# First norm's modulation: the last four of sixteen row tiles of quarters two to four multiplied and summed on TensorE

## The reference, cut to what matters

```
mod = silu(c) @ w_ada[l] + b_ada[l]            # w_ada is 2048 x 12288
shift1, scale1, gate1, shift2, scale2, gate2 = jnp.split(mod[:, None, :], 6, axis=-1)
h    = rmsnorm(x, norm_mix_g[l]) * (1 + scale1) + shift1
proj = h @ w_in[l]
```

## Time and profile before

| | |
|---|---|
| median of 3 runs | 2436.21 us (2435.95 to 2436.79) |
| profiled execution, its own time | 2439.67 us |
| its span in the profile | 2437.8 us |
| mean granted clock of TensorE | 0.97 |
| PE busy | 2305.4 us (95%), weight loads 1919.4 us (79%) |
| DVE busy | 964.6 us (40%) |
| ACT, POOL busy | 716.3 us (29%), 926.5 us (38%) |
| DMA | 355.46 MB, mean 146 GB/s |

### The profile page before, as it was taken

One profiled execution on the slowest core, in us unless ns is written; L12 is line 12 of the kernel. 1 busy time (PEld: TensorE's weight loads), 2 busy tenths in 40 slices (PEclk: granted clock), 3 DMA queues, 4 the chain that ended last, 5 costly groups with the idle time before them and its releaser, 6 DMA issues.

```text
span 2437.8 us, 27141 instructions
## 1 busy us (share of the span) xinstructions
PE 2305.4 (95%) x10448; PEld 1919.4 (79%) x10448; DVE 964.6 (40%) x1380; ACT 716.3 (29%) x980; POOL 926.5 (38%) x438
## 2 busy tenths in 40 slices
PE   3778899899998899999999999999999999999999
PEld 3667778687886788788888888888888888888887
DVE  5869886656524467496211012011021021111112
ACT  3134343433335422232122122222132231221221
POOL 1013333243431154344444444444444444444442
PEclk7889999999998999899999999999999999999999
DMA  9865445454536377256333333322333322333332
GB/s 339 308 231 168 152 160 177 167 193 156 217 104 241 108 290 259 87 201 239 107 101 96 95 95 97 100 95 95 95 95 103 95 95 95 95 103 95 95 113 78
DMA packets 188701, 355.46 MB, mean 146 GB/s; under 512 B 13258, under 2 KB 40396, under 8 KB 187344
## 3 DMA queue, kind: packets, MB, share of 16 engines
q1 hardware_dynamic: 179840, 331.34, 40.7%
q10 hardware_dynamic: 8784, 23.07, 2.5%
HBM read 327.09 MB, written 27.28 MB: 145 GB/s over the span
## 4 chain that ended last, share of the span: by engine, by line
PE 80%; DVE 10%; issue 3%; DMA 3%; ACT 2%; SPq 1%; POOL 1%; ACTq 0%; DVEq 0%; POOLq 0%
PE ps L681 26%; PE ps L683 26%; PE ps L682 25%; DVE acc L1550 2%; DVE yc L1723 2%; DVE accx L1675 1%; DMA araw<-in_w_ada 1%; PE ps L715 1%; DMA wraw<-in_w_in 1%; DMA arawx<-in_w_ada 1%; DMA gb<-g_d 0%; DMA mk<-qk_d 0%; ACTq L1244 0%; DVE utmp L1565 0%; PE ps L895 0%
## 5 line engine op out<-in xcount | busy, mean ns | idle before, releaser
L309 POOL TENSOR_TENSOR wlo<-wraw,whi 128x1024 fp32r<-128x1024 f32 (+2 forms) x372 | 893.1, 2404 | 1314.2 <-ACT whi L304 1306.0
L304 ACT ACTIVATE whi<-wraw 128x1024 fp32r<-128x1024 f32 x376 | 391.8, 1046 | 1235.6 <-PE ps L683 1182.6
L681 PE MATMUL ps<-h2T,whi 128*128 128x512 f32 x1024 | 399.8, 390 | 2.5 <-DVE h2T L2049 2.5
L682 PE MATMUL ps<-h2T,whi 128*128 128x512 f32 x1024 | 399.4, 390 | 0.0
L683 PE MATMUL ps<-h2T,wlo 128*128 128x512 f32 x1024 | 399.3, 390 | 0.0
L681 PE MATMUL ps<-ah,whi 128*128 128x512 f32 x1024 | 398.9, 390 | 0.0
L683 PE MATMUL ps<-ah,wlo 128*128 128x512 f32 x1024 | 398.4, 389 | 0.0
L682 PE MATMUL ps<-al,whi 128*128 128x512 f32 x1024 | 398.4, 389 | 0.0
L2074 DVE TENSOR_TENSOR sq<-utmp 128x512 f32<-128x512 f32 x64 | 71.9, 1142 | 561.3 <-ACT utmp L1487 550.9
L2096 DVE SCALAR_TENSOR_TENSOR x1T<-ps,M,x1T 128x512 f32<-128x512 f32 x128 | 87.5, 744 | 512.7 <-PE ps L683 512.7
L1550 DVE SCALAR_TENSOR_TENSOR acc<-araw,silc,acc 128x512 f32<-128x512 f32 x240 | 227.2, 1008 | 18.0 <-DMA araw<-in_w_ada 17.9
(11 more groups left out here) (284 smaller groups left out, 2582.7 us busy)
## 6 DMA issues: line engine op xcount, KB each, us to landing
wraw<-in_w_ff SPq DMA_DIRECT2D x256, 512.0 KB, 3.6
araw<-in_w_ada SPq DMA_DIRECT2D x128, 512.0 KB, 5.9
wraw<-in_w_in SPq DMA_DIRECT2D x72, 512.0 KB, 6.6
arawx<-in_w_ada SPq DMA_DIRECT2D x64, 512.0 KB, 4.1
wraw<-in_w_out SPq DMA_DIRECT2D x32, 512.0 KB, 6.9
xnat<-in_x ACTq DMA_DIRECT2D x4, 1024.0 KB, 8.3
xT_d<-xT ACTq DMA_DIRECT2D x1, 4096.0 KB, 13.3
qk_d<-sth ACTq DMA_DIRECT2D x16, 256.0 KB, 2.6
```

The source lines that it names most:

```text
L304: act.activation(whi[:, slot, 0:kb, 0:cols], wraw[:, slot, 0:kb, 0:cols], ACT.Copy).then_inc(hi_ready, 1)
L309: pool.tensor_tensor(wlo[:, slot, 0:kb, 0:cols], wraw[:, slot, 0:kb, 0:cols], whi[:, slot, 0:kb, 0:cols].bitcast(F), ALU.subtract).then_in ...
L681: pe.matmul(dst, lhs[0], rhs[0], start=start, stop=False)
L682: pe.matmul(dst, lhs[0], rhs[1], start=False, stop=False)
```

## The change

For the second, third and fourth quarter (q = 1, 2, 3) the row tiles 12 to 15, that is the units of u2 = 6 and 7, are no longer taken by DVE. A new function `ada_products` on PE takes them as they lie in `araw`: each 128 by 128 piece is the weight operand, the matching column of `silc` the moving one, and four row tiles accumulate into one output column. These are 2 (w) x 4 (column groups of 128) x 4 (row tiles) = 32 matmuls a quarter, into columns 8 to 15 of bank 7. They stand behind the waits for `ada_read` and `kv_part` and ahead of `ada_sum`, which stays with its eight matmuls into columns 0 to 7. DVE adds both groups of eight columns to the bias in two dependent instructions, each over shift and scale together, where two independent ones stood.

A quarter now has 24 steps on DVE in place of 32 for q = 1 to 3, and all counts of `ada_step` behind it are shifted (`ada_steps_to`). The slots of units 12 to 15 of the second and third quarter are now free only when PE has read them, so that the loads of units 4 to 7 of the third and fourth quarter wait for `ada_summed` of the quarter before.

```
--- before.py
+++ after.py
@@ -309,9 +309,17 @@
         pool.tensor_tensor(wlo[:, slot, 0:kb, 0:cols], wraw[:, slot, 0:kb, 0:cols],
                            whi[:, slot, 0:kb, 0:cols].bitcast(F), ALU.subtract).then_inc(lo_ready, 1)
 
+    def ada_steps_to(pair):
+
+        return 32 * pair - 8 * min(max(pair - 1, 0), 3)
+
     def ada_unit_release(pair, u):
 
-        return 32 * pair + 4 * (u // 2) + 3 + u % 2
+        return ada_steps_to(pair) + 4 * (u // 2) + 3 + u % 2
+
+    def by_products(pair, u2):
+
+        return pair in (1, 2, 3) and u2 >= 6
 
 
 
@@ -364,7 +372,9 @@
         sp.dma_start(wgate[:, :, :], w_in3[:, :, DIN - 16:DIN]).then_inc(gate_loaded, 16)
 
         def ada_load(pair, u, col0, col1, slots, raw, loaded):
-            if u >= slots:
+            if 4 <= u < slots and pair in (2, 3):
+                sp.wait_ge(ada_summed, pair)
+            elif u >= slots:
                 sp.wait_ge(ada_step, ada_unit_release(pair, u - slots))
             elif not (isinstance(pair, int) and pair == 0):
                 sp.wait_ge(ada_step, ada_unit_release(pair - 1, u + 16 - slots))
@@ -399,7 +409,7 @@
         def ada_unit(d):
 
             for w in range(2):
-                sp.wait_ge(ada_step, 128 + (4 * (d - 1) + 3 + w if d else 0))
+                sp.wait_ge(ada_step, ada_steps_to(4) + (4 * (d - 1) + 3 + w if d else 0))
                 if d == 0:
                     sp.wait_ge(ada_summed, 4)
                 k0 = 2 * (d % 8)
@@ -492,7 +502,7 @@
         sp.wait_ge(blk_done, q_at(PAIRS - 1) + 2)
         heads_load(0)
         pair_fills(PAIRS - 1, 10, PAIR_FILLS + 1)
-        sp.wait_ge(ada_step, 32 * 8)
+        sp.wait_ge(ada_step, ada_steps_to(8))
         sp.wait_ge(g_stored, 16)
         rows_load(0)
         for s in range(2):
@@ -707,9 +717,20 @@
                                      [act_of(i, kt) for i in range(2)], first, last)
             ins.then_inc(blk_done, 1)
 
+        def ada_products(pair, bank):
+
+            for w in range(2):
+                for u2 in (6, 7):
+                    pe.wait_ge(ada_loaded[(2 * u2 + w) % 8], 16 * (2 * pair + 2))
+                for j in range(4):
+                    for kt in range(12, KT):
+                        pe.matmul(ps[:, bank, 8 + 4 * w + j:9 + 4 * w + j],
+                                        araw[:, (2 * (kt // 2) + w) % 8, kt % 2, j * P:(j + 1) * P],
+                                        silc[:, kt:kt + 1], start=(kt == 12), stop=(kt == KT - 1))
+
         def ada_sum(pair, tile, bank):
 
-            pe.wait_ge(ada_step, 32 * (pair + 1))
+            pe.wait_ge(ada_step, ada_steps_to(pair + 1))
             for w in range(2):
                 for j in range(4):
                     ins = pe.matmul(ps[:, bank, 4 * w + j:4 * w + j + 1],
@@ -750,6 +771,7 @@
             if q >= 1:
                 pe.wait_ge(ada_read, 2 * q)
                 pe.wait_ge(kv_part, q)
+                ada_products(q, 7)
             ada_sum(q, acc[:, 2 * (q % 2):2 * (q % 2) + 2, :], 7)
             for n in range(4 * q, 4 * q + 4):
                 g, b = first_block(n)
@@ -1546,7 +1568,7 @@
                                 dve.wait_ge(ada_summed, pair - 1)
                             dve.tensor_scalar(dst, src, silc[:, kt:kt + 1], None, ALU.mult).then_inc(ada_step, 1)
                         else:
-                            dve.wait_ge(ada_step, 32 * pair + i - 1)
+                            dve.wait_ge(ada_step, ada_steps_to(pair) + i - 1)
                             dve.scalar_tensor_tensor(dst, src, silc[:, kt:kt + 1], dst, ALU.mult, ALU.add
                                                      ).then_inc(ada_step, 1)
 
@@ -1581,7 +1603,8 @@
 
 
         def quarter_units(q, us):
-            ada_units(q, us, araw, acc[:, 2 * (q % 2):2 * (q % 2) + 2, :], 8)
+            ada_units(q, [u2 for u2 in us if not by_products(q, u2)], araw,
+                      acc[:, 2 * (q % 2):2 * (q % 2) + 2, :], 8)
         def first_lo(n):
 
             cols = 336 if first_block(n)[0] == 1 else 512
@@ -1611,7 +1634,15 @@
                 kv_quarter(q - 1).then_inc(kv_part, 1)
                 quarter_units(q, range(7, 8))
                 first_lo(4 * q + 2)
-            ada_cols(q, 7, M_SH1 + 4 * q, M_SC1 + 4 * q)
+            if q >= 1:
+                dve.wait_ge(ada_summed, q + 1)
+                both = lambda tile, at: tile[:, at:at + 32].rearrange("p (w n) -> p w n", w=2)[:, :, 4 * q:4 * q + 4]
+                sums = [ps[:, 7, 8 * i:8 * i + 8].rearrange("p (w n) -> p w n", w=2) for i in range(2)]
+                dve.tensor_tensor(both(M, 0), sums[0], both(VT, V_ADA), ALU.add).then_inc(ada_read, 1)
+                dve.wait_ge(ada_read, 2 * q + 1)
+                dve.tensor_tensor(both(M, 0), sums[1], both(M, 0), ALU.add).then_inc(ada_read, 1)
+            else:
+                ada_cols(q, 7, M_SH1, M_SC1)
             dve.wait_ge(ada_read, 2 * (q + 1))
             link(dve.scalar_tensor_tensor(A1[:, 4 * q:4 * q + 4], M[:, M_SC1 + 4 * q:M_SC1 + 4 * q + 4], 1.0,
                                           VT[:, V_GMIX + 4 * q:V_GMIX + 4 * q + 4], ALU.add, ALU.mult))
@@ -1663,7 +1694,7 @@
             for kk in range(2):
                 for w in range(2):
                     kt = 2 * (d % 8) + kk
-                    step_no = 128 + 4 * d + 2 * kk + w
+                    step_no = ada_steps_to(4) + 4 * d + 2 * kk + w
                     if kk == 0:
                         dve.wait_ge(ada_loaded[w], 16 * (8 + d + 1))
                     src, dst = arawx[:, w, kk, :], accx[:, w, :]
```

## The result

| | before | changed |
|---|---|---|
| median | 2437.55 us (6 runs, 2435.95 to 2441.53) | 2453.28 us (6 runs, 2450.73 to 2461.12) |
| ratio, 95% interval | | 1.0068 (1.0049 to 1.0088) |
| profiled execution, its own time | 2439.67 us | 2451.86 us |
| its span | 2437.8 us | 2449.8 us |
| mean granted clock of TensorE | 0.97 | 0.967 |

The changed kernel is 15.7 us slower by the medians; by the ratio's interval the difference is 12 to 21 us. The forecast was 2455 us (19 us slower), the range 2442 to 2463. Two executions beside the experiments, one of the kernel before (3354.85 us, mean granted clock 0.649) and one of the kernel with the products ahead of the copy (3944.8 us, 0.554), ran in a slow state and are in no ratio.

What follows compares the result with a forecast made beforehand. DVE's closed loop was taken to bound the stage. Copy 0.64, products 11.75, sum 3.54 and small terms make 16.1 us, 6.5 more a quarter, 19.6 for three, taken as 19: 2436.2 + 19 = 2455.2 us, range 2442 to 2463.

Steps and rivals of the forecast that it cites:

- DVE bounds the stage, and the closed loop carries everything: Quarters two to four: DVE loops in 34.05 us from reading to reading, so any gain or loss counts three times.
- Nothing hides the products: In three quarters PE's products start after DVE's copy out of bank 7, at about 78.5, 112.55 and 146.6, in series.
- The price of a record: One record of a new one-column matmul on PE takes 0.106 us at clock 1.00, 0.221 us at 0.50.
- The clock falls inside the products: In each changed quarter 2.25 us run at full clock (21 records), then 43 records at 0.221: products 11.75 us.
- The difference for the stage: From the copy's start to the reading of the sums, 6.5 us more a quarter, 19.6 us for three, taken as 19.
- Carried to the end at full size: Behind the fourth quarter, blocks on PE and heads wait in the same order, so all 19 us reach the kernel's end.
- Loads at no cost: Loads of units 4 to 7 wait for the sum before, yet cost DVE only 0 to 1 us a quarter.
- The held clock: Rival: clock 1.00 through products and sum, 0.2 us gained a quarter, 2.7 us together, 2433.5 us; chance 0.13.
- the rule on short pauses between bursts: Trainium skill's claim for PE: short pauses between bursts of matmuls keep the clock up; by it the held clock would win.
- The late load: Rival: units 4 to 7 cost DVE 1 to 2 us in two quarters, 2457 to 2459 us; chance within 0.76.
- Half clock from the first product: Rival: all 64 records of a quarter at half clock, 14.2 us, 27 us more in all, 2463 us; chance 0.07.

Runs made afterwards that it cites:

- the burst without a pause in front: Changed kernel with its 32 matmuls a quarter moved ahead of the wait for `kv_part` and the copy out of bank 7: 2446.92 us, 1.0036 to the kernel before.
- the fillers: Changed kernel with seven 128-column transposes of the identity behind each group of four products, 56 a quarter: 2484.89 us, 1.0201 to the kernel before.
- two-tile experiment: Kernel before with row tiles 0 and 1 of quarters two to four on PE, between the first and second weight block of the quarter before: 2441.11 us, 1.0015.
- third-pair kernel: Kernel before with row tiles 4 and 5 of quarters two to four on PE, between two weight blocks of the quarter before: 2431.67 us, 0.9965.
- the last kernel: Third-pair kernel with 20 transposes behind each sum, 40 behind the first, and 70 before the broadcast of the norm: 2430.83 us, 0.9964 to the kernel before.

## Why the prediction was right, step by step

- **DVE bounds the stage, and the closed loop carries everything.** Right. Without the products the loop closes at 27.2 us.
- **Nothing hides the products.** Right: they start at 78.24 and 117.84, 0.6 us after the start of the copy (0.64 in the sum), with DVE idle beside them but for a low half of a weight block. The copy comes 24.66 us after a reading (117.24 - 92.58), 24.5 forecast.
- **The price of a record.** Right. With 0.106 us a record up to the clock's fall, the rest of the 64 records come out at 0.216 to 0.228 us each in the three quarters, against the 0.221 us read from the sum. The sum itself took 3.55 us.
- **The clock falls inside the products.** Right in kind, and shown: by the burst without a pause in front, and by the fillers that hold it in two quarters of three. The moment was a mean of a scatter. The products lasted 10.8, 12.6 and 10.0 us up to the sum, 11.1 on average, where the sum had 11.75; the clock fell 3.2, 1.1 and 4.0 us after their start (0.71 in 81:82, 0.99 in 118:119, 0.67 in 163:164), where I took 2.25 each time. I had carried over when it fell in the kernel before, though the readings shift against it.
- **The difference for the stage.** 19.6 us forecast (19 taken), 17.6 us found at the stage's end, 2 us of it from the term above.
- **Carried to the end at full size.** Neither refuted nor shown. 17.6 us at the stage's end were 12.0 us at the end of the profiled span and 15.7 us by the medians, and the interval of 12 to 21 us takes in the 17.6 and the 19 alike. The rest of the program varies by more than 8 us between traces, and the prediction put no term and no width for that. That 2453.28 lies within 2 us of 2455.2 is in part luck: the difference was 3.3 us too large, and the six runs of the kernel before have a median 1.3 us above that of the three that the sum started from.
- **Loads at no cost.** Right. The four loads that wait for the sum are issued from 92.58 to 94.5 and land within 6.9 us, by 101.4, and DVE starts on them at 104.37 without a pause. In the two-tile experiment, where another pair of slots came free late, DVE did wait.
- **The rivals.** The held clock didn't come about, and the rule on short pauses between bursts failed at the same place: PE's pause before the products was 1.0 to 2.3 us, and with none at all the clock fell too. The late load wasn't there. Half clock from the first product came near in the third quarter only.

## What to carry to other kernels

In this stage, work moved from the busy engine to the idle one could gain only where it ran while the busy one still worked. The wait for the copy out of bank 7 pinned it into the gap, and 36.8 us of products and slower sums stood in for 15.9 us of DVE. Before one-column matmuls are put on TensorE, ask how long a burst of them is (32 records between wide matmuls ran at or near full speed, 64 did not), what runs behind it (behind those 32 records the wide matmuls ran at half clock for 3 to 7 us in all six quarters of the two-tile and the third-pair kernel), and whose slots they free late. And look at the short serial steps on PE that already sit behind a pause: keeping the clock up there gave 1.6 us a time with no work moved.

## What the runs showed of the hardware

- Matmuls with one output column and 128x128 float32 weights keep PE at 100% busy and still let the granted clock fall to 0.50; in 120:130 it stayed there for 10 us of them. A record of this form then costs 0.22 us against 0.106 us at 1.00.
- A burst of 32 such records between wide matmuls ran at 1.00 nearly to its end, and the clock fell there, within 1.5 us of its end, in eight quarters of twelve; in the other four, all of them in the two kernels with transposes behind each sum, it stayed at 1.00.
- Transposes with 128 columns lift the clock and hold it (the fillers above; in the last kernel 70 of them ran from 32.5 us, and the clock rose inside 36:37). The Trainium skill, "TensorE: Matmul & The Clock Gate", section "Part 4: PE-mode transpose", says that transposes don't count as activity in that way; here the measurement decides against it, for float32 transposes of 128 columns, which the profile lists as MATMUL (it does not show a mode).
- A mix of half one-column matmuls and half such transposes held a clock of 1.00 for 13 us in two quarters and did not lift one of 0.50 in 22 us of the fourth.
